# Two more 1 MB places for expert weights in a two-layer decoder step

## The reference

```python
for i in range(DEPTH):                                   # 2 layers
    hn = rmsnorm(h, norm_mix[i])
    mix = conformer_conv(hn, ...) if i % 2 == 0 else mla_mixer(hn, ...)
    h = h + mix
    h = h + hier_moe(rmsnorm(h, norm_ffn[i]), ...)       # 32 experts, 2 per token
    h = h + (p[i] @ ple_w_in[i]) * sigmoid(rmsnorm(h, ple_g[i]) @ ple_w_gate[i])
return rmsnorm(h, norm_final), ...

# hier_moe, all experts: a, u: (tokens, 32, 256)
a = einsum('btd,edf->btef', h, w_gate); u = einsum('btd,edf->btef', h, w_up)
return einsum('btef,efd->btd', silu(a) * u * gates[..., None], w_down)
```

## Time and profile before

| | us |
|---|---|
| median of three runs (792.7, 794.77, 796.37) | 794.77 |
| span of the profiled execution | 790.0 |
| TensorE busy in the span | 731.0 |
| VectorE, ScalarE, GpSimd busy | 341.6, 204.8, 55.0 |

### The profile page before, as it was taken

One profiled execution on the slowest core, in us unless ns is written; L12 is line 12 of the kernel. 1 busy time (PEld: TensorE's weight loads), 2 busy tenths in 40 slices (PEclk: granted clock), 3 DMA queues, 4 the chain that ended last, 5 costly groups with the idle time before them and its releaser, 6 DMA issues.

```text
span 790.0 us, 16349 instructions
## 1 busy us (share of the span) xinstructions
PE 731.0 (93%) x6292; PEld 523.9 (66%) x6292; DVE 341.6 (43%) x1014; ACT 204.8 (26%) x499; POOL 55.0 (7%) x99
## 2 busy tenths in 40 slices
PE   9999999999999679899999999999999997688994
PEld 7886677666676446658876567777766665365583
DVE  2688624433333113235456865253333332233355
ACT  2200323421112101132235653145222121111232
POOL 2401000000000000000052630000000000000000
PEclk9999999999999989999999999999999998999997
DMA  8972995999999999999268775999999999999801
GB/s 331 395 243 72 311 426 207 390 424 420 426 428 426 423 431 424 414 421 402 111 214 288 249 226 203 427 428 376 393 423 428 425 429 423 427 430 413 344 1 55
DMA packets 48769, 271.18 MB, mean 343 GB/s; under 512 B 6817, under 2 KB 17265, under 8 KB 28465
## 3 DMA queue, kind: packets, MB, share of 16 engines
q1 hardware_dynamic: 41520, 258.50, 80.6%
q10 hardware_dynamic: 4272, 6.88, 2.6%
q0 software_dynamic: 2896, 4.72, 1.9%
HBM read 262.71 MB, written 3.88 MB: 337 GB/s over the span
## 4 chain that ended last, share of the span: by engine, by line
PE 47%; DMA 21%; DVE 4%; SPq 4%; issue 3%; ACT 2%; POOL 0%; POOLq 0%; ACTq 0%; DVEq 0%
PE bank L652 13%; DMA ring<-in_moe_w_gate_up 11%; PE bank L816 11%; DMA arena<-in_moe_w_gate_up 6%; PE bank L772 6%; PE bank L845 4%; DMA arena<-in_moe_w_down 4%; PE bank L859 3%; SPq L2337 2%; SPq L2341 2%; PE bank L789 1%; PE bank L1153 1%; PE bank L586 1%; PE bank L988 1%; PE bank L870 1%
## 5 line engine op out<-in xcount | busy, mean ns | idle before, releaser
L816 PE MATMUL bank<-ring,arena 128*32 128x256 f32 x1344 | 109.2, 399 | 16.9 <-DMA ring<-in_moe_w_gate_up 13.8
L652 PE MATMUL bank<-arena,ring 128*128 128x264 f32 (+1 forms) x440 | 102.4, 388 | 0.3 <-DVE arena L1690 0.3
L652 PE MATMUL bank<-xn_sq,ring 128*128 128x264 f32 x448 | 100.9, 386 | 0.0
L816 PEld LDWEIGHTS bank<-ring,arena 128*32 128x32 f32 x1344 | 58.5, 115 | 56.5 <-issue 33.2
L1537 DVE TENSOR_TENSOR arena<-arena,bank 128x128 f32<-128x128 f32 x34 | 9.8, 288 | 197.6 <-ACT arena L1995 197.6
L652 PEld LDWEIGHTS bank<-xn_sq,ring 128*128 128x128 f32 x448 | 85.0, 190 | 15.3 <-issue 0.9
L652 PEld LDWEIGHTS bank<-arena,ring 128*128 128x128 f32 x440 | 82.8, 190 | 17.2 <-issue 3.0
L772 PEld LDWEIGHTS bank<-arena 128*128 128x128 f32 x768 | 87.9, 192 | 8.3 <-issue 8.3
L772 PE MATMUL bank<-arena 128*128 128x128 f32 (+1 forms) x768 | 91.2, 277 | 0.0
L1555 DVE TENSOR_TENSOR hT<-hT,bank 128x264 f32<-128x264 f32 x144 | 61.6, 429 | 20.6 <-PE bank L870 11.8
L859 PE MATMUL bank<-arena 128*128 128x264 f32 x256 | 63.6, 393 | 3.0 <-issue 3.0
(11 more groups left out here) (293 smaller groups left out, 888.9 us busy)
## 6 DMA issues: line engine op xcount, KB each, us to landing
ring<-in_moe_w_gate_up SPq DMA_DIRECT2D x32, 2048.0 KB, 18.7
ring<-in_stream SPq DMA_DIRECT2D x34, 1024.0 KB, 13.8
arena<-in_moe_w_gate_up SPq DMA_DIRECT2D x14, 2048.0 KB, 24.3
ring<-in_moe_w_down SPq DMA_DIRECT2D x26, 1024.0 KB, 21.3
arena<-in_moe_w_down SPq DMA_DIRECT2D x26, 1024.0 KB, 22.1
xn_sq<-in_moe_w_gate_up SPq DMA_DIRECT2D x12, 2048.0 KB, 20.9
ring<-in_moe_w_gate_up SPq DMA_DIRECT2D x12, 1024.0 KB, 22.8
shelf<-in_moe_w_down SPq DMA_DIRECT2D x8, 1024.0 KB, 22.1
```

The source lines that it names most:

```text
L652: t = mm(ps[:, 0:cols], lhs(k), rhs(k), start=(k == 0), stop=(k == n - 1))
L816: t = mm(bank[2 + r][p0:p0 + U, 0:F].rearrange("p (c f) -> p c f", c=2), x, w[i][:, :, k * F + c * P:k * F + (c + 1) * P], start=(k == 0), ...
```

## The change

Two places more, `spare` (numbers 20 and 21), take a gate and an up matrix as a sixth pair of places, `UNIT_D`. Expert 6's gate and up move from the head of `MOE_LATE` to `MOE_STATIC`, and SyncE issues them far ahead: in layer 0 behind the shifted copies of p = 2, in layer 1 behind the fill of `G_UQ`. The later experts go round six pairs of places instead of five, with expert 9's gate and up ahead of the down weights of 8 to 10. The down weights keep their seven places.

The room comes from several tiles: the software queue's scratch is set to 2,048 bytes of a partition, the router's bias is kept for one layer at a time (layer 1's is loaded in `embed(0)`, one more transfer on ScalarE), small router tiles are packed into one, `windows` lies in another tile, and a constant is dropped (its subtraction becomes a compare and subtract in one instruction of VectorE, with signs turned in the next ones).

```diff
-ARENA = 23000
+ARENA = 22936
+SWDGE_RING = 2048
+UNIT_D = (20, 21)
-    _gu = (_r[0], _r[1], UNIT_A, UNIT_B, _r[2])
-    _dn = (SHELF, PARK, *(x[2] for x in _gu))
-    _u += [(*_gu[x % 5][0:2], _dn[x % len(_dn)]) for x in range(E - NFIRST)]
+    _gu = (UNIT_D, _r[0], _r[1], UNIT_A, UNIT_B, _r[2])
+    _dn = (SHELF, PARK, *(x[2] for x in _gu[1:]))
+    _u += [(*_gu[x % len(_gu)][0:2], _dn[x % len(_dn)]) for x in range(E - NFIRST)]
-MOE_STATIC = RING_FIRST + BESIDE + BEHIND_MEANS + RING_NEXT + [IN_PARK, IN_SHELF] + IN_NORMS + [RING_LAST]
-MOE_LATE = [[(6, 0), (6, 1), (7, 0), (7, 1), (8, 0), (8, 1), (8, 2), (9, 2), (10, 2), (9, 0), (9, 1)],
+IN_SPARE = [(6, 0), (6, 1)]
+MOE_STATIC = IN_SPARE + RING_FIRST + BESIDE + BEHIND_MEANS + RING_NEXT + [IN_PARK, IN_SHELF] + IN_NORMS + [RING_LAST]
+MOE_LATE = [[(7, 0), (7, 1), (8, 0), (8, 1), (9, 0), (9, 1), (8, 2), (9, 2), (10, 2)] for _ in range(2)]
+        spare = sb("spare", [P, 2, SLOT])
-        br = sb("br", [P, 2, GP + E])
+        br = sb("br", [P, GP + E])
-                step(v.tensor_tensor(swap[:], swap[:], cst[:, C_LAST:C_LAST + E], ALU.subtract))
+                step(v.scalar_tensor_tensor(out=swap[:], in0=iota, scalar=float(E - 1), in1=swap[:], op0=ALU.is_equal,
+                                            op1=ALU.subtract))
@@ act, embed, at l == 0 and m == 2
                         act.dma_start(wr, a["w_router"][:, 1]).then_inc(s_wr, 16)
+                        act.dma_start(br[:], a["b_router"][:, 1]).then_inc(s_wr, 16)
                         act.dma_start(pT[:], a["pT"][:, 1]).then_inc(s_p, 16)
@@ sp, the loop over p that issues the shifted copies
+                if p == PAIRS - 2:
+                    load_expert(0, *IN_SPARE[0], IN_SPARE[0][0])
             copied(sp, PAIRS - 1)
             expert_stream(0)
@@ sp, between the layers
             for g in range(G_PG0 + 2, G_UQ + 1):
                 fill(g)
+            load_expert(1, *IN_SPARE[0], IN_SPARE[0][0])
             sp.wait_ge(s_pg, 16)
-    nc = bacc.Bacc("TRN2", target_bir_lowering=False, num_devices=1)
+    nc = bacc.Bacc("TRN2", target_bir_lowering=False, num_devices=1, dynamic_dma_scratch_size=SWDGE_RING)
```

More of the change, by code:

```diff
@@ L305, in build @@
         gatesT, q = place(q, 2, T)
-        park, _ = place(q, SLOT)
-        pin1, q = place(q, KD, T)
+        pin1, _ = place(q, KD, T)
+        park, q = place(q, SLOT)
         aside, q = place(q, 5, SLOT)
@@ L314, in build @@
         rt = {}
-        for name, n in (("L", GP + E), ("gmx", 8), ("emx", 8), ("M", E), ("pos", E), ("ex", 5), ("gsum", 1),
-                        ("den", 1), ("w", 2), ("slots", 2), ("near", 2), ("ge", E), ("code", 2), ("own", 2),
-                        ("home", 2), ("over", 2), ("first", 2)):
+        for name, n in (("L", GP + E), ("gmx", 8), ("emx", 8), ("M", E), ("pos", E), ("ge", E)):
             rt[name] = sb("rt_" + name, [P, 3, n])
+        narrow = [("ex", 5), ("gsum", 1), ("den", 1), ("w", 2), ("slots", 2), ("near", 2), ("code", 2), ("own", 2),
+                  ("home", 2), ("over", 2), ("first", 2)]
+        columns = sb("rt_columns", [P, 3 * sum(n for _, n in narrow) + 7])
+        col = 0
+        for name, n in narrow:
+            rt[name] = columns[:, col:col + 3 * n].rearrange("p (i n) -> p i n", i=3)
+            col += 3 * n
+        rcol = columns[:, col:col + 3]
+        busiest, shift_by, most = (columns[:, col + 3 + i:col + 4 + i] for i in range(3))
+        early_root = columns[0:1, col + 6:col + 7]
         M12, both = (sb("rt_" + name, [P, 2, 3, E]) for name in ("M12", "both"))
@@ L334, in build @@
         perm = sb("perm", [P, E])
-        most = sb("most", [P, 1])
         permI = sb("permI", [P, E], I32)
         mostI = sb("mostI", [P, 1], I32)
-        windows = sb("windows", [P, NWIN])
+        windows = O[:, 1, 0:NWIN]
         windowsI = sb("windowsI", [P, NWIN], I32)
@@ L407, in build @@
         signalled = {PLACE[p] for p in LOADS}
-        w_in = [sem(f"w_in{i}") if i in signalled else None for i in range(PARK + 1)]
+        w_in = [sem(f"w_in{i}") if i in signalled else None for i in range(NPLACE)]
         s_x = [sem("in_" + n) for n in ("x0_then_p", "x1_then_router", "x2", "x3")]
@@ L516, in slot @@
                 return ring[:, i, :]
+            if i >= UNIT_D[0]:
+                return spare[:, i - UNIT_D[0], :]
             if i >= SHELF:
@@ L529, in expert_gu @@
                 return ring[:, i:i + 2, :]
+            if i == UNIT_D[0]:
+                return spare[:]
             return aside[:, 0:2, :] if i < 14 else aside_x if i < 16 else in_turn
@@ L1446, in all_slots @@
                 freed(dve, key)
[L1447 to L1451, removed]
[L1452 to L1453 removed]
+                step(v.max(late8, late[:]))
+                step(v.max_index(late_ix, late8, late[:]))
+                step(v.tensor_copy(busiest, late_ix[:, 0:1]))
+                v.tensor_scalar(swap[:], iota, busiest, None, ALU.is_equal)
+                step(v.tensor_scalar(shift_by, busiest, float(U), -PLACES[E - 1], ALU.mult, ALU.add))
+                step(v.scalar_tensor_tensor(out=swap[:], in0=iota, scalar=float(E - 1), in1=swap[:], op0=ALU.is_equal,
+                                            op1=ALU.subtract))
+                v.scalar_tensor_tensor(out=base[:], in0=swap[:], scalar=shift_by, in1=cst[:, C_BASE:C_BASE + E],
                                        op0=ALU.mult, op1=ALU.add)
[L1455 removed]
+                step(v.scalar_tensor_tensor(out=cap[:], in0=swap[:], scalar=-float(U), in1=cst[:, C_CAP:C_CAP + E],
                                             op0=ALU.mult, op1=ALU.add))
@@ L1480, in weights_and_order @@
                 v.tensor_tensor(late[:], cnt[:], cap[:], ALU.subtract)
-                step(v.tensor_scalar(shift_by[:], busiest[:], -1.0, float(E - 1), ALU.mult, ALU.add))
-                v.scalar_tensor_tensor(out=perm[:], in0=swap[:], scalar=shift_by[:], in1=iota, op0=ALU.mult,
+                step(v.tensor_scalar(shift_by, busiest, 1.0, -float(E - 1), ALU.mult, ALU.add))
+                v.scalar_tensor_tensor(out=perm[:], in0=swap[:], scalar=shift_by, in1=iota, op0=ALU.mult,
                                        op1=ALU.add)
-                step(v.reduce_max(most[:], late[:], AX.X))
-                step(v.tensor_scalar(most[:], most[:], float(-U), 0.0, ALU.add, ALU.max))
-                v.tensor_copy(mostI[:], most[:])
+                step(v.reduce_max(most, late[:], AX.X))
+                step(v.tensor_scalar(most, most, float(-U), 0.0, ALU.add, ALU.max))
+                v.tensor_copy(mostI[:], most)
                 v.tensor_copy(permI[:], perm[:]).then_inc(s_perm, 1)
```

42 lines of the change are left out of this document (17 added, 25 removed).

## The result

The changed kernel takes 784.88 us (median of four executions, 782.03 to 788.02), against 794.63 us for the kernel before beside it. The measured ratio is 0.9847, with a 95% interval of 0.9806 to 0.9888; the two medians alone give 0.9877, inside it. Of the 794.63 us beside it the ratio makes 782.5. The forecast was 785.5.

A forecast was written before the change was run, and what follows sets the result against it. It took the expert stages as bound by full DMA engines loading weights. 790.0 - 9.9 (early loads) + 0.6 (bias) = 780.7 us of span, plus 4.8 to the median, gave 785.5 us; range 782.5 to 790.5.

The forecast's parts named there:

- Six pairs of places instead of five: Expert stages: SyncE may issue one expert earlier, closing only small DMA dips; counted 0, at most 0.4 us a layer.
- The bound and the formula: Expert stages: the end is the end of `gate_up(0)` plus the bytes still to load / 424 GB/s.
- The 4.95 us a layer: Expert stages: 2.097 MB of expert 6's gate and up moved ahead, at 0.4235 MB/us; 9.9 us in both layers.
- drain at each turn: Rival: GpSimd waits for its transfers at the smaller ring's end; 788.8 us, chance 0.04; in several places 791 to 795, 0.06.
- throttle: Rival: GpSimd waits for queue room at each rotary key issue; 815 us with two in flight; chance 0.06.
- one layer only: Rival: one early transfer delays layer 0's copies of p = 3 or a layer 1 fill; 790.4 us, chance 0.10.
- no effect: Rival: the expert stage doesn't shorten because the gap at 148 us grows by what was saved; 795.4 us, chance 0.04.
- (1): Gate and up transfers into `spare` at about 59 and 347 us, with DMA share near 1 between 60 and 66 us.
- (2): Layer 0: the copies of p = 3 still start at 72.4 us.
- (3): Layer 0's last down product at 336.8 instead of 341.7 us.
- (4): TensorE's waits for gate and up weights, then at line 816, fall from 29 to about 19 us.
- (5): TensorE's wait at 383.4 us, now near 378.4, is about 0.9 us instead of 0.28.

The follow-up runs named there:

- e8_fills: Changed kernel with layer 1's router bias loaded by SyncE, plus seven constant products before each weight wait in pairs 10 to 15: 791.51 us, ratio 0.9949.
- e2_layer0_only: Changed kernel, but layer 1's expert 6 gate and up go back behind expert 7's; only layer 0 loads early: 790.21 us, ratio 0.9914.
- e4_five_pairs: Changed kernel with the early loads, but the spare places serve expert 6 alone and later experts go round five pairs: 793.75 us, ratio 0.9943.
- e10_again: Changed kernel unaltered, measured a third time: 789.66 against 796.48 us for the kernel before, ratio 0.9926.
- e1_again: Changed kernel unaltered, measured again with more rounds: 788.09 against 797.48 us for the kernel before, ratio 0.9892.

## Where the prediction was right, and where it failed

**What failed.** By the ratio the time is 782.5 us, 3.0 under the forecast and at the range's low end (written as 782.5, while its working, 785.5 - 0.8 - 1.9, gives 782.8). The mechanism of the stages held, and two steps did not. One is the term *Six pairs of places instead of five*, put at 0 to 0.4 us a layer: the sixth pair is worth 3.0 and 2.8. This did not move the time, since the change has both edits. The other is the time outside the stages. The sum held it fixed at one profile's value plus 4.8 us, and the range kept 1.9 for the spread of runs. The profiles show it anywhere between 391.4 and 400.7 us, 9.3 apart. The stages and the bias account for 8.7 us, and the first comparison shows 12.2 by its ratio (9.8 by its medians). What is left over falls to this second term, by elimination. Which executions that comparison caught stays open, since only one of its runs has a profile.

**The bound and the formula: right.** Both stages end when the last down weights land, the DMA engines are full, and the gain came out of TensorE's idle time with its busy time unchanged. TensorE's idle time stays at 15.6 and 13.6 us, and e8_fills shows what is behind the step "Does TensorE become the bound? No": it does once some 16 us are added.

**The 4.95 us a layer: nearly.** 4.2 and 4.8 came. Counted as bytes the 2.1 MB are gone: layer 0's stage moved 196.26 x 0.420 = 82.4 MB before and 192.08 x 0.418 = 80.3 after. (The 4.95 came only because the sixth pair came with it, as said below.) The formula took 424 GB/s as fixed. Without the first 7 us (306 and 300 GB/s), 80.3 MB went in 189.3 us before and 78.2 in 185.1 after: the rate is 422.5 instead of 424, and that makes 0.8 us. The two repeats give 422.5 and 422.6 by the same count. Why a rate falls by half a per cent no run tells.

**Where the early loads hide: right.** They went out at 58.56 and 342.33 us, the copies of p = 3 started at 72.20 for 72.39, the taps behind them waited 0.76 us for 0.99, and the next two fills went out at 360.60 for 365.18, which is the lead of the stage. The issue of layer 1's load took SyncE 0.38 us, not the 6.9 that were allowed for. (The "20 us of room" among the rivals stands nowhere above it; the earlier trace rows show 18 us in which the DMA engines stand.) Both prices of nothing held; e2_layer0_only shows that neither layer pays for the other.

**Six pairs of places at "0, and at most 0.4 us a layer": wrong.** With the early load the sixth pair is worth 3.0 us in layer 0 and 2.8 in layer 1 (e4_five_pairs). I read the full DMA engines as proof that places were not short. They weren't, in a trace where 2 MB more kept the engines back. Take these away, and the engines reach the places before TensorE has left them. The sentence "the pieces behind keep their issue times" has this in it unseen: the sum came out by luck, because the change has both edits, not because the step was right.

**The bias at 0.6 us: half of that**, 0.3. The issue takes 0.47 us, and some of it probably lies beside VectorE's work.

**The small queue at 0: right**, as far as a ratio tells whose interval reaches 0.2% to the slow side. The rivals of a drain at each turn and of a throttle fall: pauses of 0.28 to 0.48 us are far from 3.3, and one within the second batch is far from one an issue. The rivals of one layer only and of no effect fall by the table. VectorE's changed instruction and the packed tiles have no run of their own. But e10_again's rest, 392.5 us, is no longer than the 393.1 before, which leaves them no cost that shows.

**"The median stands 4.8 us above the profiled span": wrong.** The changed kernel's four runs have both numbers, and the difference is 1.6 to 1.7 in each (788.02 and 786.4; 782.03 and 780.4). So the profiled execution of before took about 791.6, among the fastest of that kernel, nearly all of whose runs in the later comparisons lie between 789 and 802. The other 3 us of the 4.8 are not around the span. They are probably in it in other executions: the rest of 393.1 us that this profile shows is near the least there is (391.4 to 400.7 in the table). Adding the 4.8 back was harmless for the sum, since before and after have the same scatter. It was not for the range.

**The range's low end: too near.** The runs of the changed kernel alone spread over 782 to 788 in one comparison, and over 782 to 793 on another chip (without one slower still). The interval of the ratio reaches down to 779.2 us. By the stages and the bias the change is worth 9.0 - 0.3 = 8.7 us, which is also the mean of the three differences of medians (9.8, 9.4, 6.8). What the first comparison shows beyond the forecast is then of the rest and not of the change; these runs have no profile, so that is argued.

**The list of what would show it.** (1), (2) and (3) came: 58.56, and 342.33 for the 347 written; 72.20; and 337.13 for 336.8. (4) The waits at what is now line 823 fell to 19.6 us as foreseen (below). (5) The wait is 0.58 at 378.81 us instead of 0.9. (6) The second batch ran from 438.52 to 457.11 us, 18.6 with the pause of 0.28 in it.

TensorE's waits, whole span, changed kernel (total us, times, longest us; they answer to the earlier trace rows):

```profile
PE bank L823 <- DMA ring<-in_moe_w_gate_up: 15.9, 6, 4.2
PE bank L823 <- DMA arena<-in_moe_w_gate_up: 3.7, 3, 2.0
PE bank L877 <- issue: 3.0, 2, 2.7
...
PE bank L1160 <- DMA arena<-in_cache_kpeT: 1.4, 1, 1.4
```

## What to carry to other kernels

Where a stage streams at the full rate of the DMA engines, its length is the bytes behind its start over the measured rate, and what is loaded ahead into a pause comes off it. But loading ahead and the number of buffers are one edit: the stream that has less to do at its start reaches its buffers sooner, and "the DMA engines are full" in the trace of before doesn't show that the buffers will do after (3 of the 4.2 us hung on the sixth pair here). And when one profile is laid against a median, first ask which execution the profile was; cut the kernel into stages whose length repeats, and the rest shows by itself.

## What the runs showed of the hardware

The wait behind the last down product comes in two sizes. In the 24 places of the twelve profiles it is 2.55 to 2.89 us seven times and 0.28 to 0.63 thirteen times, and four times there is none. The changed kernel has 0.35 in layer 0 and 2.67 in layer 1, its repeat e1_again has 2.73 and 2.89, and e10_again 0.28 and 0.54. The profile calls it "issue", and TensorE passes a branch there. The DMA packets of the traces tell more. Part 3 of the page counts those of one queue of instructions (packets, MB, share):

```profile
q8 instruction: 52, 0.85, 0.4%
```

They have 16 KB each and start some 10 us apart while TensorE streams. In e8_fills, with 336 more instructions on TensorE, there are 53, so they are taken here for TensorE's instructions. In all 20 waits the first product behind starts 2.63 to 2.70 us after the start of such a packet. In the long waits the packet starts within 0.2 us of the wait's start. In the short ones it starts 2.0 to 2.4 us earlier, while products still run. So what TensorE waits for is very probably its instructions. The Trainium skill, "Runtime: NRT & Kernel Launch", section "Instruction fetch mechanics", says that a taken branch to code outside the instruction window has to fetch it first. The packets agree with that, but no run here moved the branch. Why the packet starts late in some executions stays open.

The scatter between executions lies outside the stages, and the profiles show two things in it. One is the long wait: the rest is 391.4 to 395.0 us in the six profiles without one, 396.1 to 398.5 in the five with one, and 400.7 in the one with two. The other is the granted clock. In the changed kernel it fell to 0.50, the level of 1.2 GHz, in 740 to 745 us, behind 2.67 us in which TensorE stood. In e10_again, with 0.54 us there, it stayed at 1.00. Of the seven long waits four have such a fall behind them, and of the 17 other places none. In all, some 10 us of TensorE's work outside the stages ran at 0.50 in the changed kernel's profile, which is about 5 us lost (an estimate, from the half speed), and none in e10_again's.

The falls inside the expert stages stand behind waits for weights, and no run shows that they cost anything: the stages end on the landing of the last weights. With those waits filled the clock stays at 1.00 and the time gets worse (e8_fills).

A software queue scratch of 2,048 bytes carried 64 transfers of 16 KB in two batches with single pauses of 0.15 to 0.38 us inside them (the kernel before has one of 0.38 too), and gave part of the room for the two places.
